# Reordered norms between the stages of a one-step decoder trunk

## What is computed

```python
mod = (silu_c @ p['w_ada'][l] + p['b_ada'][l]).reshape(B, N_MOD, D)
hh = modulate(rmsnorm(x, p['g_pre'][l, 0]), m[0], m[1])
f = swiglu(hh, p['w_ffn_gate'][l, 0], p['w_ffn_up'][l, 0], p['w_ffn_down'][l, 0])
x = x + 0.5 * m[2] * rmsnorm(f, p['g_post'][l, 0])
hh = modulate(rmsnorm(x, p['g_pre'][l, 1]), m[3], m[4])
```

## Time and profile before

| | |
|---|---|
| runs | 1508.42 us median of 3 (1507.28 to 1508.64) |
| profiled execution | 1509.57 us, of it 1507.9 us span |
| PE, PEld busy | 1413.2 us (94%), 1294.3 us (86%) |
| DVE, ACT, POOL busy | 809.4 us (54%), 610.7 us (41%), 99.7 us (7%) |
| mean granted TensorE clock | 0.942 |
| sums of tokens L1552 | 192 matmuls of one column, 233 ns each |

### The profile page before, as it was taken

The page is one execution under the profiler, slowest core; times in us unless marked ns, Lnnn a source line. Parts: engine busy times, 40 slices in busy tenths (PEclk is TensorE's granted clock), DMA queues, the critical chain, the costliest instruction groups (busy, mean ns, idle before and its releaser), DMA issues.

```text
span 1507.9 us, 24340 instructions
## 1 busy us (share of the span) xinstructions
PE 1413.2 (94%) x9758; PEld 1294.3 (86%) x9758; DVE 809.4 (54%) x1488; ACT 610.7 (41%) x1033; POOL 99.7 (7%) x144
## 2 busy tenths in 40 slices
PE   5899999989889899999999999999999798999997
PEld 1799999979775587999999799999979487999996
DVE  1644444576764557444445644444567876444444
ACT  2533334443331244433344443343445664343432
POOL 0000000031001102000000200000020201000000
PEclk8799999999996968999999899999989898999998
DMA  9566655465365636365444646534464643444342
GB/s 366 176 208 201 206 167 188 152 199 176 106 241 201 212 128 201 120 208 182 141 143 142 218 142 207 178 127 136 162 228 145 248 143 108 141 142 148 121 149 91
DMA packets 82195, 260.07 MB, mean 172 GB/s; under 512 B 11570, under 2 KB 22898, under 8 KB 81970
## 3 DMA queue, kind: packets, MB, share of 16 engines
q1 hardware_dynamic: 65618, 199.56, 39.8%
q0 software_dynamic: 16480, 59.15, 11.5%
HBM read 254.45 MB, written 4.23 MB: 172 GB/s over the span
## 4 chain that ended last, share of the span: by engine, by line
PE 85%; DVE 8%; ACT 3%; DMA 2%; issue 1%; SPq 0%; DVEq 0%; ACTq 0%
PE ps L1469 25%; PE ps L1471 24%; PE ps L1470 24%; PE ps L1531 3%; PE ps L1552 1%; PE ps L790 1%; DVE w_lo L1903 1%; DMA x<-in_x 1%; DMA a_raw<-in_ada 1%; DMA lent_lo<-in_ada 1%; DVE f L1986 1%; DVE f L1966 1%; PE ps L1560 1%; PE ps L1545 1%; PE ps L713 1%
## 5 line engine op out<-in xcount | busy, mean ns | idle before, releaser
L1469 PE MATMUL ps<-xn_hi,w_hi 128*128 128x320 f32 x1872 | 597.0, 319 | 23.6 <-DVE xn_lo L1978 14.9
L1470 PE MATMUL ps<-xn_lo,w_hi 128*128 128x320 f32 x1872 | 584.6, 312 | 0.0
L1471 PE MATMUL ps<-xn_hi,w_lo 128*128 128x320 f32 x1872 | 584.5, 312 | 0.0
L1903 DVE TENSOR_TENSOR w_lo<-w_raw,w_hi 128x1024 fp32r<-128x1024 f32 x352 | 375.7, 1107 | 134.5 <-ACT w_hi L1713 134.1
L1469 PEld LDWEIGHTS ps<-xn_hi,w_hi 128*128 128x128 f32 x1872 | 357.0, 191 | 55.0 <-issue 45.8
L1713 ACT ACTIVATE w_hi<-w_raw 128x1024 fp32r<-128x1024 f32 x362 | 331.1, 961 | 93.3 <-PE ps L1471 84.4
L1470 PEld LDWEIGHTS ps<-xn_lo,w_hi 128*128 128x128 f32 x1872 | 357.7, 191 | 1.2
L1471 PEld LDWEIGHTS ps<-xn_hi,w_lo 128*128 128x128 f32 x1872 | 357.1, 191 | 0.0
L1469 PE MATMUL ps<-mid_hi,w_hi 128*128 128x320 f32 x704 | 218.2, 310 | 0.3 <-DVE w_lo L1903 0.3
L1471 PE MATMUL ps<-mid_hi,w_lo 128*128 128x320 f32 x704 | 217.4, 309 | 0.0
L1470 PE MATMUL ps<-mid_lo,w_hi 128*128 128x320 f32 x704 | 217.4, 309 | 0.0
(11 more groups left out here) (273 smaller groups left out, 960.9 us busy)
## 6 DMA issues: line engine op xcount, KB each, us to landing
w_raw<-in_gu SPq DMA_DIRECT2D x176, 512.0 KB, 4.5
a_raw<-in_ada POOLq DMA_DIRECT2D x96, 512.0 KB, 4.7
w_raw<-in_down SPq DMA_DIRECT2D x64, 512.0 KB, 3.6
w_raw<-in_pj SPq DMA_DIRECT2D x58, 512.0 KB, 5.0
w_raw<-in_down SPq DMA_DIRECT2D x64, 192.0 KB, 3.6
a_raw<-in_ada SPq DMA_DIRECT2D x16, 512.0 KB, 7.9
w_raw<-in_ada SPq DMA_DIRECT2D x16, 512.0 KB, 5.8
lent_hi<-in_ada SPq DMA_DIRECT2D x8, 512.0 KB, 8.6
```

The lines of the kernel that those rows point to most:

```text
L1469: pe.matmul(out, hi, xhi, start=start, stop=False)
L1470: pe.matmul(out, hi, xlo, start=False, stop=False)
L1471: return pe.matmul(out, w_lo[s][:, w_at:w_at + P], xhi, start=False, stop=stop)
L1903: dve.tensor_tensor(w_lo[s][:, cols], w_raw[:, s, cols], w_hi[s][:, cols].bitcast(F32), ALU.subtract).then_inc(w_split, 1)
```

## The change

- Plan of pieces: "sum" and ("first", 1) are gone; "root" 2, "spread" 3, ("first", 2) 3.
- TensorE: y's sums first, then its root; y's spread before the last moments; after `down`, the sums of ff_sum are issued within the last half tile of `down`. All sums are 64 columns wide instead of one (`WIDE`), with readers taking every 64th column.
- ScalarE: the square of y before the copy of f (a semaphore f_copied now releases VectorE's part); the last `square_f` behind `root_y`; in a gate a Silu of one element and the row's copy ahead of w_hi.
- TensorE transposes the row right after the two tiles by the new turn (gate, 0), which before was (gate, 1).
- VectorE: growths 0, 1, 2 before `mean_square`, 3 behind it, 4 behind the inverse; its intermediate results go to PSUM; then additions, two at a time; scale and shift per chunk for chunks 0 and 1. The second half of the next tile's low part moves from GpSimd to VectorE, between low(2) and low(3).

```diff
-    return [(stage, "sum", 1), (stage, "root", 2), (stage, "spread", 2), (stage, ("first", 1), 1),
-            (stage, ("first", 2), 2)]
+    return [(stage, "root", 2), (stage, "spread", 3), (stage, ("first", 2), 3)]
...
-             ("attention", 0): [5, 6, 7, 8, 9], ("gate1", 1): [10], ("gate1", 13): [11], ("gate2", 1): [12],
-             ("gate2", 13): [13], ("odd_tail", 0): [14], ("odd_out", 0): [15, 16], ("gate3", 1): [17]}
+             ("attention", 0): [5, 6, 7, 8, 9], ("gate1", 0): [10], ("gate1", 13): [11], ("gate2", 0): [12],
+             ("gate2", 13): [13], ("odd_tail", 0): [14], ("odd_out", 0): [15, 16], ("gate3", 0): [17]}
...
+WIDE = 64
...
             low_ahead(gp, stage, 0)
             ada_load(gp, pieces[A_SLOTS + 1:KC])
-            low_ahead(gp, stage, 1)
...
-                    last = pe.matmul(ps[0:TN, bank, col + c:col + c + 1], src[:, c0:c0 + TN], ones_d[:, 0:1],
+                    at_ = WIDE * (col + c)
+                    last = pe.matmul(ps[0:TN, bank, at_:at_ + WIDE], src[:, c0:c0 + TN], ones_d[:, 0:WIDE],
...
+            def ff_sums(stage):
+
+                pe.wait_ge(ff_added, 6 * (SUB[stage] + 1))
+                token_sums(B_MOMENTS, NTC, sums_of(stage)["ff_sum"], True, False)
+
             def stats(stage, prep):
 
                 w, q = sums_of(stage), 8 * SUB[stage]
-                pe.wait_ge(xf_added, 7 * (SUB[stage] + 1))
-                token_sums(B_MOMENTS, 0, w["xf_sum"], True, False)
-                pe.wait_ge(ff_added, 6 * (SUB[stage] + 1))
-                token_sums(B_MOMENTS, NTC, w["ff_sum"], False, False)
                 pe.wait_ge(y_evac, CR + q + 7)
                 token_sums(B_YSUM, 0, sqacc[:, :], True, False)
-                ada_pieces(prep, "sum")
                 pe.wait_ge(sq_ready, q + 8)
                 token_sums(B_YSUM, 0, sq2[:, 1, :], False, True).then_inc(stat_done, 1)
+                if stage.startswith("down"):
+                    pe.wait_ge(xf_added, 7 * (SUB[stage] + 1))
+                    token_sums(B_MOMENTS, 0, w["xf_sum"], False, False)
+                    spread(y_stat(stage), ry3, B_RY)
+                else:
+                    spread(y_stat(stage), ry3, B_RY)
+                    ff_sums(stage)
+                    pe.wait_ge(xf_added, 7 * (SUB[stage] + 1))
+                    token_sums(B_MOMENTS, 0, w["xf_sum"], False, False)
                 pe.wait_ge(xf_ready, SUB[stage] + 1)
                 token_sums(B_MOMENTS, 0, w["xf"], False, False)
                 pe.wait_ge(ff_ready, q + 8)
                 token_sums(B_MOMENTS, NTC, w["ff"][:, 1, :], False, True).then_inc(moments_done, 1)
-                spread(y_stat(stage), ry3, B_RY)
                 ada_pieces(prep, "root")
...
-                        ada_transpose(stage, 1)
+                        ada_transpose(stage, 0)
...
+                            if end and j == 3 and ff < N_FFN - 1:
+                                ff_sums(stage)
...
                 root_y(stage)
+                square_f(stage, KC - 1)
                 ahead(prep, (0,))
...
+                            act.activation(warm[:, :], eps[:, :], ACT.Silu)
+                            ada_copy(*turns(stage, 0))
...
-                act.activation(at(f, m)[:, 0:PTOK], ps[:, b, 0:PTOK], ACT.Copy,
-                               scale=gate_of(stage, m)[:, 0:1])
                 first = isinstance(m, int) and m == 0
                 act.activation(sqacc[:, :] if first else sq2[:, b, :], ps[:, b, 0:TOK], ACT.Square).then_inc(sq_ready, 1)
+                act.activation(at(f, m)[:, 0:PTOK], ps[:, b, 0:PTOK], ACT.Copy,
+                               scale=gate_of(stage, m)[:, 0:1]).then_inc(f_copied, 1)
...
-                m_xf, m_ff = ps[0:TN, B_MOMENTS, 0:NTC], ps[0:TN, B_MOMENTS, NTC:2 * NTC]
+                m_xf, m_ff = ps[0:TN, B_MOMENTS, 0:WIDE * NTC:WIDE], ps[0:TN, B_MOMENTS, WIDE * NTC:2 * WIDE * NTC:WIDE]
+                p3 = ps[0:TN, B_MOMENTS, 512 - NTC:512]
                 dve.wait_ge(moments_done, SUB[stage] + 1)
                 dve.wait_ge(rstd_ready, y_stat(stage))
                 steps.did(dve.tensor_tensor(s3[:, :], m_ff, ry3[:, :], ALU.mult))
                 steps.wait()
-                steps.did(dve.scalar_tensor_tensor(s3[:, :], m_xf, 2.0, s3[:, :], ALU.mult, ALU.add))
+                steps.did(dve.scalar_tensor_tensor(p3, m_xf, 2.0, s3[:, :], ALU.mult, ALU.add))
                 steps.wait()
-                steps.did(dve.tensor_tensor(s3[:, :], s3[:, :], ry3[:, :], ALU.mult))
+                steps.did(dve.tensor_tensor(p3, p3, ry3[:, :], ALU.mult))
                 steps.wait()
-                steps.did(dve.tensor_tensor(s3[:, :], s3[:, :], mean_x[:, :], ALU.add))
+                steps.did(dve.tensor_tensor(p3, p3, mean_x[:, :], ALU.add))
                 steps.wait()
-                dve.tensor_scalar(mean_x[:, :], s3[:, :], 0.0, None, ALU.max).then_inc(mean_ready, 1)
+                dve.tensor_scalar(mean_x[:, :], p3, 0.0, None, ALU.max).then_inc(mean_ready, 1)
...
-                def scaled(*ks):
-                    k0, k1 = ks[0], ks[-1] + 1
-                    for k in ks:
-                        if sub:
-                            dve.wait_ge(x_ready, 8 * (sub - 1) + k + 1)
-                        dve.tensor_tensor(f[:, k, :], x[:, k, :], ps[:, B_RX if sub else B_RY, 0:TOK],
+                def scaled(k):
+                    if sub:
+                        dve.wait_ge(x_ready, 8 * (sub - 1) + k + 1)
+                    dve.tensor_tensor(f[:, k, :], x[:, k, :], ps[:, B_RX if sub else B_RY, 0:TOK],
                                   ALU.mult).then_inc(xr_ready, 1)
-                    fs = f[:, k0:k1, PTOK:TOK].rearrange("p k (b t) -> p k b t", b=NB)
-                    each = lambda at_: modT[:, at_(sub, k0):at_(sub, k0) + len(ks), 1:NCOND].unsqueeze(3)\
-                        .to_broadcast([P, len(ks), NB, NT])
-                    dve.wait_ge(xr_ready, 8 * sub + k1)
-                    steps.did(dve.tensor_tensor(fs, fs, each(scale_at), ALU.mult))
+
+                def samples(at_, op, k0, n):
+                    fs = f[:, k0:k0 + n, PTOK:TOK].rearrange("p k (b t) -> p k b t", b=NB)
+                    each = modT[:, at_(sub, k0):at_(sub, k0) + n, 1:NCOND].unsqueeze(3).to_broadcast([P, n, NB, NT])
+                    return dve.tensor_tensor(fs, fs, each, op)
+
+                def sample_scale(k0, n=1):
+                    dve.wait_ge(xr_ready, 8 * sub + k0 + n)
+                    steps.did(samples(scale_at, ALU.mult, k0, n))
+
+                def sample_shift(k0, n=1):
                     steps.wait()
-                    dve.tensor_tensor(fs, fs, each(shift_at), ALU.add).then_inc(xmod_ready, len(ks))
-
-                def grow_and_low(pair, lows):
-                    for k, l in zip(pair, lows):
-                        if sub:
+                    samples(shift_at, ALU.add, k0, n).then_inc(xmod_ready, n)
+
+                def pair(k):
+                    scaled(k)
+                    scaled(k + 1)
+                    sample_scale(k, 2)
+                    sample_shift(k, 2)
+
+                def residual(*ks):
+                    if sub:
+                        for k in ks:
+                            add(k)
+
+                def grown(*ks):
+                    if sub:
+                        for k in ks:
                             grow(k)
-                        low(l)
-                        if sub:
-                            add(k)
 
                 if sub:
                     dve.wait_ge(r_ready, y_stat(stage))
-                    grow(0)
-                    grow(1)
-                    add(0)
+                    grown(0, 1, 2)
+                    mean_square(stage, prep)
+                    grown(3)
                     invert(x_stat(prep), rx3)
-                    add(1)
+                    grown(4)
                 else:
-                    dve.tensor_copy(mean_x[:, :], ps[0:TN, B_YSUM, 0:NTC])
+                    dve.tensor_copy(mean_x[:, :], ps[0:TN, B_YSUM, 0:WIDE * NTC:WIDE])
+                residual(0, 1)
                 dve.wait_ge(r_ready, x_stat(prep))
                 scaled(0)
+                sample_scale(0)
+                sample_shift(0)
                 scaled(1)
-                grow_and_low((2, 3), (0, 1))
+                sample_scale(1)
+                sample_shift(1)
+                low(0)
+                residual(2, 3)
+                low(1)
                 if not sub:
                     ahead(prep, (0,))
-                scaled(2, 3)
-                grow_and_low((4, 5), (2, 3))
-                if not sub:
-                    ahead(prep, (1,))
-                scaled(4, 5)
-                grow_and_low((6, 7), (4, 5))
-                scaled(6, 7)
+                pair(2)
+                low(2)
+                if sub:
+                    dve.wait_ge(w_split, CR + 2 * W_BASE[prep] + 3)
+                ahead(prep, (1,))
+                low(3)
```

(21 more changed lines are left out.)

4 lines of the change are left out of this document (2 added, 2 removed).

## The result

The changed kernel takes 1495.14 us (median of four runs, 1493.85 to 1498.56) against 1508.32 for the kernel before beside it: a ratio of 0.9903, 95% interval 0.9882 to 0.9923, so 13.2 us less where 7.3 were forecast. The sign and most of the mechanisms were right; the gain was nearly twice as large.

What follows compares the result with a forecast made beforehand. TensorE was taken to bound the kernel, 85% of the chain that ended last. Terms -0.7 - 3.0 - 5.85 + 2.2 gave -7.3 us (rounded), so a median of 1501.1 us, range 1491 to 1507.

Steps and rivals of the forecast that it cites:

- T - E: Stage's last product (E) to VectorE scaling x's first chunk (T): 9.1 us after `down`, 10.4 after projections; -0.7 in sum.
- The half behind piece 6: In each norm GpSimd's half split follows the load of piece 6, from M + 1.5 to M + 3.85 (M: moments' end).
- the group of 64 columns: Six TensorE instructions for a wide sum in the norms, taken at 0.66 us between bounds 0.56 and 0.83.
- The root of y: In the norm after `down`, the root of y was to start about 1.75 us after the stage's last product.
- rival B: The TensorE clock holds in even_out's norm, giving 1498.9 us; chance 0.12.
- The clock after even_out: In the norm after even_out, TensorE's clock falls to the half level as before, costing +2.2 us.
- Rival D: TensorE's clock falls from 2 us after the stage's last product in every norm: 10.5 us, so 1511.7; chance 0.08.
- From T on: From VectorE's first scaling of x to the end of the first two tiles: 21.35 us everywhere, -3.0 over five norms.
- The third tile: In three gates TensorE no longer waits for ada_row before the third tile: 3 x -1.95 = -5.85 us.
- Rival C: The gates' third tile waits for something else, say VectorE: +5.85, 1507 us; chance 0.08.
- the third step at 0.17: VectorE's third step of the mean square in the norm takes 0.16 to 0.2 us, where it took 2.14.
- the stretched additions: In each norm VectorE's addition 0 is stretched to the end of GpSimd's half split.

## Why the prediction was off, step by step

- **T - E, the chain of steps: right in form, terms mis-sized, -2.2.** The half behind piece 6, the additions held by it, and T about 4.7 behind the end of the moments came as written (measured 4.6). One reading was off on both sides: E was set 0.09 to 0.17 too early, which made T - E of before too long (10.2 for 10.06 and so on, 0.7 in all) and the way to y's last group as well (ScalarE's first evacuation is at E + 0.20, not 0.33). In the difference the two cancel. What is left is 2.4 us, less 0.1 of rounding. The largest term in it is the group of 64 columns: taken at 0.66, "a little under the line" between 0.56 and 0.83, measured 0.53 behind a spread and 0.57 behind another group, and no more with 84 columns than 0.55 and 0.57. Behind y's spread the groups took 1.19 instead of 1.32 us after `down` and 2.32 instead of 2.64 after a projection, and the moved ones 0.58 instead of 0.66: 3 x 0.13 + 2 x 0.32 + 3 x 0.08 = 1.3 us. Another 0.4 is y's spread, which took 0.75 instead of 0.83 in all five norms, and 0.65 lies between the end of the moments and T, 4.57 instead of 4.7. The root of y came at E + 1.50 instead of 1.75, half of that by the shift of E. The choice should have gone to the lower bound: the spread differs from the groups in its weights too, and a line between two rows that differ in two things is no interpolation. The rule of the Trainium skill that the prediction set beside it ("TensorE: Matmul & The Clock Gate", "Back-to-back issue gap": one price from 1 to 64 columns) described it better; it puts the median at 1498.9, and with rival B as well at 1496.7.
- **The clock after even_out: wrong, -2.2.** The step that failed is "I take the fall there as it was, since TensorE does less than before", a term of +2.2 in the sum. In its place the clock stayed at 1.00 from E to T, and T - E was 9.69. The experiments with 1 and 16 columns lose the clock there, those with 64 and 84 do not, at equal order and equal waits; rival B, 0.12, is what happened. TensorE was busy for 8.0 us of the stretch instead of 11.2 and kept the clock, so comparing busy time did not foretell it. Rival D, the same fear in all norms, is close to what the changed kernel does with one column, where the clock falls from E + 3.2 to 3.8 in four of five norms; with 64 it doesn't.
- **From T on: right, 0.7 too good.** 21.35 was forecast, 21.32 to 21.34 measured. The ends of two tiles before, taken from idle times, were read 0.15 to 0.2 too late: -3.0 instead of -2.3. That a slow clock at the first products no longer adds to it came as written, though in before those products run slowly for 6 us in gate1, gate2 and odd_in alone; in gate3 it is 3.4.
- **The third tile: right in place, 0.6 too small.** The transposes take 0.36 behind the two tiles, while in before "third" was 2.52: 2.15 per gate instead of 1.95. This is the error of the line above once more, with the other sign: an end of the two tiles that is put too late shortens the wait behind it. hbuf, named as late next, was in time. Rival C has no trace.
- **Missed altogether: the clock behind gate3's wait, -1.5, and in the last norm, -0.6.** The wait was costed without what it did to the products behind it, though the windows behind 1273.52 could have been read before. The last norm was taken at 0; its spread at the half level goes with narrow sums: 1.62, 1.37 and 1.62 in three of four profiles with 1 or 16 columns, 0.92 in all eight with 64 or 84.
- Terms of zero: the wait for the last addition to ff_sum and piece 7 landing later show no cost in the trace; the part ahead of the first norm varies by more than 1 us from one profiled execution to the next, so its term can't be told. (The norm before gate1 lasts 13.8 us in before, outside the 13.3 to 13.6 that the prediction read; nothing rests on that.)

The errors are -2.2, -2.2, -2.1 and -0.6 against +0.7, together -6.4, and the forecast of -7.3 becomes, within 0.1, the -13.8 that the stretches show, beside -13.2 by the medians. Little of it is luck in either direction: the +0.7 and the -0.6 are mostly one boundary read late, and the other three all leaned to the slow side. The sign and the mechanisms of most terms were forecast, the size was not. Of the predicted signs in the profile, the third step at 0.17, the stretched additions, the end at T + 21.3 and the missing waits at the gates came; T - E missed by 0.4 to 0.5 and by 0.7, the root of y by 0.25.

## What to carry to other kernels

A wait of TensorE between stages has two prices, its own length and the clock behind it, so read the granted clock of the stretch after every wait that a change removes or adds. Where TensorE must do short work between waits, make it wide if width is free: read the distance between the starts of a narrow group and a wide one, and the clock behind both. And when two engines hold each other up, look first at what their queues put ahead of the operation: here exchanging two lines of one queue brought 9.1 us in the norms, two thirds of what the whole change did, and made the detour through PSUM worth 2.3.

## What was not expected of the hardware

- Six fp32 matmuls with 107-wide weights, directly behind six others, cost 0.57 us for 1, 16, 64 or 84 columns each, at the full clock, and 1.08 at the half level (seen with 1 and 16).
- At equal instructions and waits, 1 or 16 columns let the granted clock fall to 0.50 between E and T in seven of ten norms, and 64 or 84 kept it at 1.00 in all 35, worth 0.6 to 2.3 us in a norm.
- Of six waits of 1.93 to 1.98 us between long runs of products, in two kernels, three were followed by 3.4 us at 1.2 GHz, and three by none.
